# Padding between the K tiles of the turned activations in a two-layer block

## What is computed

```
h = rms_norm(x) ; proj = h @ w_in          # 1024 x 8280: gated delta rule, indexed attention, gates
x = x + merged @ w_out
x = x + square(relu(rms_norm(x) @ w_mlp_up)) @ w_mlp_down         # 4096 wide
h = x ; h = h + concat(retention, forgetting attention) @ w_out_2 # from rmsnorm(h) @ w_in_2
h = h + cross_attention(rmsnorm(h), mem)                          # w_xq, w_xkv, w_xo
h = h + (silu(hn @ w_gate) * (hn @ w_up)) @ w_down                # 2816 wide
```

## Time and profile before

| | |
|---|---|
| median of 3 runs | 901.51 us (901.18 to 901.99) |
| the profiled execution | 902.32 us |
| its span in the profile | 900.5 us |
| TensorE matmul busy | 889.2 us (99% of the span) |
| TensorE weight load busy | 764.4 us (85%) |
| VectorE busy | 587.0 us (65%) |
| ScalarE busy | 447.9 us (50%) |
| GpSimd busy | 113.0 us (13%) |
| HBM read | 147.59 MB, 166 GB/s over the span |

### The profile page before, as it was taken

The page is one execution under the profiler, slowest core; times in us unless marked ns, Lnnn a source line. Parts: engine busy times, 40 slices in busy tenths (PEclk is TensorE's granted clock), DMA queues, the critical chain, the costliest instruction groups (busy, mean ns, idle before and its releaser), DMA issues.

```text
span 900.5 us, 12630 instructions
## 1 busy us (share of the span) xinstructions
PE 889.2 (99%) x5035; PEld 764.4 (85%) x5035; DVE 587.0 (65%) x850; ACT 447.9 (50%) x631; POOL 113.0 (13%) x84
## 2 busy tenths in 40 slices
PE   9999999999999999999999999999999999999998
PEld 6887787888978999988888889888888888888886
DVE  5478978997787566645355747977785565555542
ACT  6265456854535555543345335646554544444531
POOL 0431225665110000000000002100100000000200
PEclk9999999999999999999999999999999999999999
DMA  8874542344225555566568635533542565554562
GB/s 289 203 250 142 186 140 69 126 142 120 95 95 187 158 181 182 182 193 201 199 194 282 203 102 193 170 111 104 178 139 91 166 200 183 186 179 136 196 230 70
DMA packets 83554, 149.74 MB, mean 166 GB/s; under 512 B 8480, under 2 KB 16208, under 8 KB 83376
## 3 DMA queue, kind: packets, MB, share of 16 engines
q1 hardware_dynamic: 80352, 144.55, 49.4%
q10 hardware_dynamic: 2528, 3.63, 1.1%
q0 software_dynamic: 624, 0.87, 0.8%
HBM read 147.59 MB, written 1.44 MB: 166 GB/s over the span
## 4 chain that ended last, share of the span: by engine, by line
PE 87%; DVE 7%; DMA 3%; ACT 1%; issue 1%; POOL 0%; SPq 0%; DVEq 0%; ACTq 0%; POOLq 0%
PE gemm L497 64%; PE mixbank L991 5%; PE gemm L991 5%; DMA raw<-in_w_in_dram 2%; DVE w_lo L1823 2%; PE mixbank L560 1%; PE mixbank L657 1%; PE mixbank L682 1%; DMA x<-in_x_dram 1%; PE mixbank L852 1%; PE mixbank L1163 1%; DVE mix L1944 1%; PE gemm L1191 1%; PE mixbank L668 1%; ACT w_hi L1270 1%
## 5 line engine op out<-in xcount | busy, mean ns | idle before, releaser
L1823 DVE TENSOR_TENSOR w_lo<-raw,w_hi 128x2048 fp32r<-128x2048 f32 (+3 forms) x131 | 284.8, 2184 | 186.0 <-ACT w_hi L1270 185.9
L1270 ACT ACTIVATE w_hi<-raw 128x2048 fp32r<-128x2048 f32 (+3 forms) x140 | 255.4, 1833 | 173.7 <-DMA raw<-in_w_in_dram 52.0
L497 PE MATMUL gemm<-w_hi,s_hi 128*128 128x512 f32 (+3 forms) x784 | 209.2, 387 | 1.0 <-issue 0.5
L497 PE MATMUL gemm<-w_lo,s_hi 128*128 128x512 f32 (+3 forms) x784 | 201.9, 377 | 1.2 <-DVE w_lo L1823 1.1
L497 PE MATMUL gemm<-w_hi,s_lo 128*128 128x512 f32 (+3 forms) x784 | 201.7, 377 | 0.0
L497 PEld LDWEIGHTS gemm<-w_lo,s_hi 128*128 128x128 f32 x784 | 142.6, 188 | 29.1 <-DVE w_lo L1823 1.9
L497 PEld LDWEIGHTS gemm<-w_hi,s_lo 128*128 128x128 f32 x784 | 142.7, 188 | 27.6
L497 PEld LDWEIGHTS gemm<-w_hi,s_hi 128*128 128x128 f32 x784 | 139.6, 188 | 27.4 <-issue 2.5
L2636 POOL TENSOR_TENSOR sm<-sm 128x2 f32<-128x2 f32 (+5 forms) x13 | 22.0, 1695 | 458.2 <-DVE sm L1867 300.9
L2630 POOL TENSOR_TENSOR w_lo<-raw,w_hi 128x2048 fp32r<-128x2048 f32 x9 | 41.3, 4606 | 157.4 <-ACT w_hi L1270 157.4
L1287 ACT ACTIVATE mix<-gemm,sm 128x512 f32<-128x512 f32 (+2 forms) x25 | 16.3, 653 | 53.7 <-PE gemm L497 53.7
(11 more groups left out here) (352 smaller groups left out, 1163.7 us busy)
## 6 DMA issues: line engine op xcount, KB each, us to landing
raw<-in_w_in_dram SPq DMA_DIRECT2D x40, 1024.0 KB, 5.1
raw<-in_w_mlp_up_dram SPq DMA_DIRECT2D x16, 1024.0 KB, 5.6
raw<-in_w_mlp_down_dram SPq DMA_DIRECT2D x16, 1024.0 KB, 5.1
raw<-in_w_gate_dram SPq DMA_DIRECT2D x10, 1024.0 KB, 5.1
raw<-in_w_up_dram SPq DMA_DIRECT2D x10, 1024.0 KB, 5.1
raw<-in_w_down_dram SPq DMA_DIRECT2D x10, 1024.0 KB, 5.1
raw<-in_w_out_dram SPq DMA_DIRECT2D x8, 1024.0 KB, 5.2
raw<-in_w_xkv_dram SPq DMA_DIRECT2D x8, 1024.0 KB, 5.1
```

What stands on the lines that cost most here:

```text
L497: return nc.tensor.matmul(G[b % 2][t][:, 0:width], lhs, rhs, start=kt == 0 and not (low_x or low_w), stop=kt == blk["kt"] - 1 and (low_x i ...
L1270: nc.scalar.activation(w_hi[:, n % SLOTS, 0:kn, 0:width], raw[:, n % SLOTS, 0:kn, 0:width], ACT.Copy)\
L1823: V.tensor_tensor(w_lo[:, s, 0:kn, 0:width], raw[:, s, 0:kn, 0:width], w_hi[:, s, 0:kn, 0:width].bitcast(F32), ALU.subtract)\
```

## The change

The two tiles get 20 more float32 elements behind each K tile, 80 bytes, and the kernel uses the first 256 elements of each as before. K tile `kt` then starts 1,104 bytes times `kt` into its tile instead of 1,024 times `kt`. Each tile is 640 bytes longer, so `s_lo` starts 640 bytes further up and all that is declared behind it 1,280 bytes. No instruction is added, removed or moved.

```diff
-        s_hi = sb("s_hi", [P, KT, SEQ], F32R)
-        s_lo = sb("s_lo", [P, KT, SEQ], F32R)
+        s_hi = sb("s_hi", [P, KT, SEQ + 20], F32R)[:, :, 0:SEQ]
+        s_lo = sb("s_lo", [P, KT, SEQ + 20], F32R)[:, :, 0:SEQ]
```

## The result

| | before | after |
|---|---|---|
| median of 3 runs | 901.51 us | 906.70 us (906.56 to 907.30) |
| the profiled execution | 902.32 us | 906.56 us |
| its span | 900.5 us | 904.8 us |
| TensorE matmul busy | 889.2 us | 895.0 us |

The change makes the kernel slower: ratio 1.0059, 95% interval 1.0043 to 1.0075, 5.2 us. The forecast was 901.6 us, no change, with a range up to 903.0.

A forecast was written before the change was run, and what follows sets the result against it. The prediction took TensorE's matmul rate to bound the kernel. Its terms, 0 + 0 + 0.05 + 0 us, left the median of 901.51 us at a forecast of 901.6 us, range 900.3 to 903.0.

The forecast's parts named there:

- What bounds the kernel: Whole kernel: the rate at which TensorE takes matmuls, busy 889.2 of 900.5 us; waits at other engines worth almost nothing.
- (c): Writers of two K tiles, lines 1294 and 1856: two stretches instead of one, 0.06 us in all, counted as 0.05 us.
- (d): `x`, constants and arena move by 1,280 bytes: taken as 0, bounds 0.1 us either way.
- Term (a): Line 497, 2,352 stationary pieces on padded tiles: address effect taken as 0, bounds 10.7 ns gain and 3.1 ns loss each.
- The arena's equal pace: Line 497: stationary pieces in the arena took 226.8 and 227.0 ns, against 226.9 on the padded tiles.
- The second witness: Line 1105, plain float32: starts at multiples of 8 bytes only, 109.1 ns against 109.4 for aligned ones at line 1045.
- the bubble of 13.4: Float32r matmuls: the part of each one's time that doesn't grow with the columns, about 13.4 ns.
- Term (b): Line 991, 768 matmuls streaming padded K tiles: only starts move, taken as 0, bounds -10.7 and +3.1 ns each.
- The share of 0.9: Lines 497 and 991: 666 of some 743 us lie on the chain, so 0.9 of a matmul change reaches the time.
- The second: Rival, lines 497 and 991: starts off 64-byte multiples cost reads 1.5 ns, 904.7 us; chance 0.05, plus 0.01 if under 0.85 ns.
- The first: Rival, lines 497 and 991: stationary and streaming reads collide, skew saves 10.7 ns per matmul, 26.3 us, to 875; chance 0.05.
- The third: Rival, other engines: TensorE unaffected, the arena's new place helps or hurts another engine, 901.5 plus or minus 0.3 us; chance 0.03.

## Why the prediction was wrong, step by step

**What bounds the kernel** was right: TensorE's pace decides, and nothing else moved. Terms (c) and (d) were right as well: lines 1294 and 1856 kept 595 and 685 ns, and moving what lies behind measured 1.0001.

**Term (a) failed**, the stationary pieces of line 497, taken at 0. It is +5.0 ns for each matmul of 512 columns on the padded tiles (22.25 / 96 = 231.8 against 21.77 / 96 = 226.8). The step that failed is the use of the witnesses. The arena's equal pace was read as a sign that the phase to the weights plays no part; its distance differs by 512 bytes, a multiple of the 256 that matters, so it was no witness at all. All distances of float32r pieces in the kernel before are multiples of 256, and its trace couldn't show this term. The second witness, line 1105 with plain float32, does have other distances and doesn't pay, before or after; that a float32r matmul would do likewise was an inference over a difference that the prediction itself had noted, the bubble of 13.4 against 2.7 ns. The upper bound of 3.1 ns was also too low. The prediction has no term, either, for the 640 bytes by which `s_lo` moves, 128 modulo 256. It made no difference here (906.92 us with `s_lo` put back, 906.70 with the change), but by itself it costs 3.3 us.

**Term (b) failed too**: line 991 gained 1.7 ns each, 1.3 us, within the bounds but taken at 0. The prediction had one hint that such a pace isn't fixed, the two blocks of 260 columns at 118.5 and 120.0 ns, and took it up in both rivals. Both blocks have distance 0, so they are no example of this term.

**The share of 0.9** was too high for the part ahead of 270 us. With the measured sizes in the prediction's own sum, 2,352 x 5.0 x 0.9 = 10.6 us less 768 x 1.7 x 0.9 = 1.2 us gives 9.4 us, where 5.2 were measured. The starts of the chain's pieces tell where the rest stayed. Before, and then after:

```profile
50.09 20.22 PE gemm L497 x108
...
270.58 16.61 PE gemm L497 x72
```

```profile
49.13 20.56 PE gemm L497 x108
...
270.40 16.92 PE gemm L497 x72
```

From 270 us on the kernel after fell from 0.2 us ahead (270.40 against 270.58) to 4.3 us behind at the last piece (846.86 against 842.60), 4.4 us, which is 5.8 us lost at line 497 less 1.3 gained at line 991 (rounded). There stand 1,320 matmuls of 512 columns on the padded tiles (2,352 less the 840 before 270 us and the 192 of 256 and 260 columns), at 5.0 ns 6.6 us, so about 0.9 of it came through. Of the 840 ahead of that little did: pieces are short there, and the path runs through VectorE and transfers in between. From the piece at 50 us to that at 270 us the kernel before takes 220.5 us and the kernel after 221.3, 0.8 us more, for 600 matmuls of 512 columns (3.0 us at 5.0 ns). The kernel after reached the first of these pieces 1.0 us sooner, which is spread of the start: kernels whose line 497 kept its pace reached it between 48.97 and 50.09 us. So 5.8 + 0.8 - 1.3 = 5.3 us, against 5.2 between the medians, and less the early start 4.3, against 4.2 between the two profiled executions (906.56 - 902.32).

**The rivals.** The second named the right sign (+3.2 us, with 6.5 as its end) for the wrong reason: 64 bytes of padding cost as much as 80, and 16 or 32 bytes of shift make line 991 faster. The first, a collision of the two reads in which both start in step, had the dependence on distance right, but the other way round at line 497, if distance 0 is what it calls in step: that is the best case there, and at other distances the part that doesn't grow with the columns goes from 13.6 to 18.5 ns on average (231.8 - 213.3). At line 991 it goes from 13.3 to 10.0 ns (116.7 - 106.7), as that rival would have it. The third, another engine helped or hurt by the arena's new place, is what the run with only the move shows to be nothing. The first two together had 0.11 of the chance, which was too little for a term of which the trace held no example.

**On the rule weighed there.** The Trainium skill, page "SBUF — State Buffer", section "Who interferes with whom", has two independent ports for the moving operand and the weight load. If that were all, the distance between the two couldn't matter; the runs with the weights moved alone (1.0045) and with everything moved (1.0002) show that it does. The figure of the Trainium skill, page "TensorE: Matmul & The Clock Gate", section "Back-to-back issue gap", for the isolated gap, 215.8 ns at 512 columns, was reached at no distance tried.

**What stays open.** That the two reads meet in the memory is an inference from the period of 256 bytes; no run shows the place where they meet. It is also open why one layout can have two paces (226.8 and 233.5 ns in the run with both tiles 16 bytes further, 233.3 and 229.0 ns with the weights moved), why 512 and 256 columns have opposite best cases, and why line 991 is at 117.8 ns with one tile at 0 and the other at 128, when either distance alone gives 120.0. And it is open what in plain float32 avoids the toll.

## What to carry to other kernels

In a float32r kernel that is bound by matmuls, the distance modulo 256 bytes between the stationary and the streaming piece was here worth 1 to 3% of a matmul, in a direction that depends on how many columns stream: keep it at 0 where 512 do, and try 16 or 32 bytes where 256 do. A change of a tile's length moves every tile behind it; work out all starts modulo 256 before an edit is read as one change, for three of these runs meant to change one distance and changed others with it. And a row that shows "no effect of the address" is a witness only for distances that it differs in.

## What the runs showed of the hardware

Not expected was a matmul pace that depends on addresses at all: 512 columns at 226.8 ns with a distance of 0 modulo 256 bytes and mostly 229 to 234 ns else, 256 columns at line 991 at 120.0 ns with all pairs at 0 or all at 128 and 116.7 to 118.9 ns else (118.9 is 11.41 / 96 in the run with the weights' tiles 16 bytes further), with the clock at its full value in all. Nor that one layout can have two paces: in the run with both tiles 16 bytes further, neighbouring pieces of 96 took 22.42 and 21.77 us. Last, the tile `phase` of 448 bytes, which nothing uses, puts the arena at 108,032 = 422 x 256 bytes from the weights; without it the distance would be 64. No run took it away.
